# Down projections of a decoder layer: low and high input halves as one 512-column moving operand

## The reference, cut to what matters

```
def swiglu(h, w_gate, w_up, w_down):
    return (jax.nn.silu(h @ w_gate) * (h @ w_up)) @ w_down

x = x + 0.5 * swiglu(rms_norm(x, norm_ffn1), ffn1_gate, ffn1_up, ffn1_down)
...    # attention and RWKV mixing between the two
x = x + 0.5 * swiglu(rms_norm(x, norm_ffn2), ffn2_gate, ffn2_up, ffn2_down)
return rms_norm(x, norm_final)
```

## Time and profile before

| | |
|---|---|
| three runs | 624.00, 624.55, 629.41 us, median 624.55 |
| span of the profiled execution | 622.4 us |
| own time of the profiled execution | not in the record; the median stands 2.15 us above the span |
| PE busy | 98% of the span |
| two down projections | about 134 to 195 us and 554 to 615 us |

### The profile page before, as it was taken

The page is one execution under the profiler, slowest core; times in us unless marked ns, Lnnn a source line. Parts: engine busy times, 40 slices in busy tenths (PEclk is TensorE's granted clock), DMA queues, the critical chain, the costliest instruction groups (busy, mean ns, idle before and its releaser), DMA issues.

```text
span 622.4 us, 15455 instructions
## 1 busy us (share of the span) xinstructions
PE 612.2 (98%) x6716; PEld 597.0 (96%) x6716; DVE 421.0 (68%) x493; ACT 296.9 (48%) x345; POOL 89.4 (14%) x90
## 2 busy tenths in 40 slices
PE   9999999999999999999999999999999999999996
PEld 8899999999999999999988889999999999999996
DVE  5757787765556369968994336977767666665663
ACT  6734555444434274434665544644644444443332
POOL 0116900000114000020005524004000000000130
PEclk9999999999999999999999999999999999999999
DMA  8677656656555345585232222365566656556551
GB/s 287 217 229 236 201 183 186 191 169 200 177 189 200 98 136 190 190 187 159 91 120 87 71 86 77 103 201 183 179 196 202 202 185 187 186 170 208 181 166 67
DMA packets 100672, 105.40 MB, mean 169 GB/s; under 512 B 2244, under 2 KB 98732, under 8 KB 100628
## 3 DMA queue, kind: packets, MB, share of 16 engines
q1 hardware_dynamic: 99380, 101.47, 50.9%
q0 software_dynamic: 1088, 3.02, 2.2%
q10 hardware_dynamic: 160, 0.27, 0.1%
HBM read 103.50 MB, written 1.25 MB: 168 GB/s over the span
## 4 chain that ended last, share of the span: by engine, by line
PE 83%; DVE 8%; ACT 4%; DMA 3%; issue 1%; SPq 0%; ACTq 0%; DVEq 0%
PE two L1467 24%; PE two L1468 23%; PE two L1469 23%; PE two L1463 10%; DVE w_lo L905 4%; ACT w_hi L532 2%; DMA w_raw<-in_ffn_up 1%; DMA w_raw<-in_ffn_down 1%; DMA w_raw<-in_ffn_gate 1%; DMA x_tok<-in_x 1%; PE two L1741 1%; PE two L1742 1%; PE two L1743 1%; DVE gates L1110 0%; PE two L1886 0%
## 5 line engine op out<-in xcount | busy, mean ns | idle before, releaser
L532 ACT ACTIVATE w_hi<-w_raw 128x2048 fp32r<-128x2048 f32 (+1 forms) x86 | 162.5, 1890 | 244.4 <-PE two L1469 214.8
L905 DVE TENSOR_TENSOR w_lo<-w_raw,w_hi 128x2048 fp32r<-128x2048 f32 (+1 forms) x86 | 199.5, 2320 | 84.0 <-ACT w_hi L532 83.7
L1467 PE MATMUL two<-hlo_f,w_hi 128*128 128x256 f32 x640 | 177.8, 278 | 1.7 <-DVE w_lo L905 1.7
L1468 PE MATMUL two<-hhi_f,w_lo 128*128 128x256 f32 x640 | 177.4, 277 | 0.0
L1469 PE MATMUL two<-hhi_f,w_hi 128*128 128x256 f32 x640 | 177.4, 277 | 0.0
L1467 PEld LDWEIGHTS two<-hlo_f,w_hi 128*128 128x128 f32 x640 | 120.8, 189 | 2.7 <-DVE w_lo L905 2.2
L1468 PEld LDWEIGHTS two<-hhi_f,w_lo 128*128 128x128 f32 x640 | 120.9, 189 | 0.0
L1469 PEld LDWEIGHTS two<-hhi_f,w_hi 128*128 128x128 f32 x640 | 120.9, 189 | 0.0
L1467 PE MATMUL two<-hid_lo_t,w_hi 128*128 128x256 f32 x352 | 97.7, 278 | 0.7
L1468 PE MATMUL two<-hid_hi_t,w_lo 128*128 128x256 f32 x352 | 97.2, 276 | 0.0
L1469 PE MATMUL two<-hid_hi_t,w_hi 128*128 128x256 f32 x352 | 97.2, 276 | 0.0
(11 more groups left out here) (344 smaller groups left out, 981.9 us busy)
## 6 DMA issues: line engine op xcount, KB each, us to landing
w_raw<-in_ffn_up SPq DMA_DIRECT2D x21, 1024.0 KB, 5.4
w_raw<-in_ffn_gate SPq DMA_DIRECT2D x20, 1024.0 KB, 5.4
w_raw<-in_w_in SPq DMA_DIRECT2D x20, 1024.0 KB, 5.0
w_raw<-in_ffn_down SPq DMA_DIRECT2D x16, 896.0 KB, 4.6
w_raw<-in_ffn_down SPq DMA_DIRECT2D x8, 1024.0 KB, 5.0
w_raw<-in_w_out SPq DMA_DIRECT2D x4, 1024.0 KB, 5.0
w_raw<-in_proj_a SPq DMA_DIRECT2D x4, 512.0 KB, 3.7
w_raw<-in_proj_b SPq DMA_DIRECT2D x4, 512.0 KB, 4.3
```

The source lines that it names most:

```text
L532: nc.scalar.activation(whi[slot][:, 0:kts], raw[slot][:, 0:kts], ACT.Copy).then_inc(sg["hi_ready"], 1)
L905: nc.vector.tensor_tensor(wlo[slot][:, 0:kts], raw[slot][:, 0:kts], whi[slot][:, 0:kts].bitcast(F32), ALU.subtract).then_inc(sg["lo_ready" ...
L1467: mm(dst, whi[slot][:, k_, cols], xl, start=start, stop=False)
L1468: mm(dst, wlo[slot][:, k_, cols], xh, start=False, stop=False)
```

## The change

`hid_hi` and `hid_lo` become the two halves of one tile, `hid_x[P, FT, 2, T]`, with the low part first. For each 128-row tile the two products with the same high weights are one product with 512 moving columns, [low | high], into the whole bank. The product of the low weights with the high input goes to the bank's second half. The bank then holds two partial sums, so DVE adds each half of the bank to the residual by an instruction of its own, the second behind a semaphore that the first raises.

```
-            hid_hi = sb("hid_hi_t", [P, FT, T], F32R, scope=sc)
-            hid_lo = sb("hid_lo_t", [P, FT, T], F32R, scope=sc)
+            hid_x = sb("hid_x", [P, FT, 2, T], F32R, scope=sc)
+            hid_lo, hid_hi = hid_x[:, :, 0], hid_x[:, :, 1]
...
                             nc.vector.scalar_tensor_tensor(out=x[:, 2 * j + m], in0=bank[2 + m][:, 0:T], scalar=0.5,
                                                            in1=x[:, 2 * j + m], op0=ALU.mult, op1=ALU.add)\
+                                .then_inc(sg["x_half"], 1)
+                            dve.wait_ge(sg["x_half"], 2 * (j + f * (D // W)) + m + 1)
+                            nc.vector.scalar_tensor_tensor(out=x[:, 2 * j + m], in0=bank[2 + m][:, T:2 * T], scalar=0.5,
+                                                           in1=x[:, 2 * j + m], op0=ALU.mult, op1=ALU.add)\
                                 .then_inc((sg["x_ffn_even"], sg["x_ffn_odd"])[m], 1)
...
                             for c in range(KS[part_]):
-                                last = three(bank[2 + m][:, 0:T], s, c, slice(m * P, (m + 1) * P),
-                                             hid_hi[:, k0 + c], hid_lo[:, k0 + c],
-                                             k0 + c == 0, k0 + c == FT - 1)
+                                cols = slice(m * P, (m + 1) * P)
+                                part(bank[2 + m], whi[s][:, c, cols], hid_x[:, k0 + c].rearrange("p a t -> p (a t)"),
+                                     k0 + c == 0)
+                                last = part(bank[2 + m][:, T:2 * T], wlo[s][:, c, cols], hid_hi[:, k0 + c])
```

More of the change, by code:

```diff
@@ L124 @@
 first_hi first_lo first_norm sq_one sq_sum last_sq mean_sq rms_ready rstd_ready gained hhi_ready hlo_ready
-gate_taken up_taken silu_done hid_prod hid_hi hid_lo down_first x_ffn_even x_ffn_odd
+gate_taken up_taken silu_done hid_prod hid_hi hid_lo down_first x_half x_ffn_even x_ffn_odd
 bias_row bias_row_sb bias_out bias_in
```

## The result

The changed kernel takes 631.2 us in the median of 6 runs (627.8 to 635.92), the kernel before 624.27 us in the same comparison (6 runs, 621.42 to 629.41). The ratio is 1.009, with a 95% interval of 1.0046 to 1.0135: 3 to 8 us slower, where 2.6 us faster was forecast. The measured time lies outside the range.

What follows compares the result with a forecast made beforehand. PE's stream was taken as the bound. Products 3.77, first chunks -0.30, second-layer stalls -1.22, first-layer stalls +0.82 and end -0.46 summed to 2.61 us faster: 624.55 to 621.9 us, range 619.8 to 626.0.

Steps and rivals of the forecast that it cites:

- What bounds the kernel: Whole kernel: PE, busy 98% of the span at full clock, holds 83% of the chain; only shortening its stream gains.
- Products: Down projections: a tile goes from 340.0 to 329.3 ns (216 plus 113.3), 3.77 us faster over 352 tiles.
- the 216 ns passes: Eight plain-float32 passes of 256 columns, 216 ns each, 2.6 over streaming; taken as the price of a 512-column product.
- the cost goes by columns: Rival, down projections: the 6.7 ns belongs to each 256 columns, products gain nothing; 0.7 us slower, 625.2; chance 0.09.
- First chunks: First layer's third chunk, stall at 143.8: PE's gain in the two chunks before is lost waiting for late weights; -0.30 us.
- Additions and what stands behind them: DVE after groups 1 and 2: direct waits hidden; first layer's stalls vanish, +0.82 us; second layer's grow, -1.22 us.
- E + 2.36: Second layer: gain multiplication's predicted end, 2.36 us after E, PE's start of the next group's part 0.
- End: End of the kernel: the new addition stands whole in the final chain; -0.46 us.
- five stalls: Late chunk starts in the down projections, some 0.41 us each: one at 143.8, four after groups 1 and 2.
- I am wrong if the two steps of a tile sum to more than 332: Down projections: forecast refuted if a tile's steps sum above 332 or below 327 ns, or first layer's stalls stay.

Runs made afterwards that it cites:

- e3: The changed kernel with its products reordered: within a part and half, first all 512-column products, then all 256-column ones; ratio to the kernel before 1.0067.
- e5: The changed kernel without the 256-column products of the low weights, so its down projections have 512-column products alone; 613.03 us in one run.
- after_again: The changed kernel, unchanged, run again for a second trace; 631.63 us in one run.
- e4: The changed kernel with the first of the two additions per half left out; ratio to the kernel before 1.0097.
- e2: The kernel before with only the second addition per half added, of 0.0 times the bank; ratio 0.9996.
- e8: The kernel before with POOL's squaring after groups 1 and 2 waiting for DVE's low part of the next group's second chunk; median 622.93 us, ratio 0.9965.
- e7: The changed kernel with 44 warm-up products after the first down projection, putting later scan instructions where the kernel before has them; 639.14 us in one run.

## Why the prediction was wrong, point by point

**What bounds the kernel:** right. PE's stream sets the time, and all that was gained or lost went through it. Only "the full clock throughout" is not quite so: the granted clock was 0.5 from 29.0 to 32.5 us, which the page's tenths don't show. The down projections ran at 1.00.

**Products: wrong, and this is the step that failed.** I took 216 ns for the wide product because it "has the shape of the 216 ns passes", and 113.3 for the narrow one. The passes in the earlier trace rows are plain float32, which spends two cycles on a column, and have 2.6 ns over their streaming time. That surplus does not carry over to float32r at one cycle per column. There the surplus grows with the columns: 13 ns at 384, and 20 to 22 in the mean at 512 in three kernels with three different neighbourhoods (e3, e5 and the change). I had this as the rival "the cost goes by columns" and gave it 0.09. Even that rival was too mild, since it kept 340 ns per tile. The wide product never went below 225 ns, two at the lower price, and mostly took 235, two products at the higher price; and the narrow one beside it took 118. The tile is 353 instead of 329.3, and 352 tiles cost 352 x 13 = 4.6 us where a gain of 3.77 was booked. The records of 512 columns are 397 ns long, not 380.

The surplus of 6.7 ns which I read as a loss between two equally long activities is the lower of two prices of 256 columns. The first trace happens to show the lower one in nearly all long stretches, so the step looked like a constant. In all twelve traces a stream of 256-column products changes between the two prices only at a break: a late start, another shape, or, in after_again at 50.4 us, a single step of 124 ns. The unbroken stream behind it keeps its price, and the mixed stream of the change is at the higher one but for single wide products right behind a break.

The Trainium skill ("TensorE: Matmul & The Clock Gate", section Back-to-back issue gap) has N / 2.4 + 2.5 for an isolated product, 215.8 ns for 512 columns. The float32 passes of the earlier trace rows, with the same 213.3 ns of streaming, come near it at 216. No float32r product here does; the least that any kernel showed for 512 columns is 225.

**First chunks:** the term (-0.30) assumed a gain to lose. In the first trace the late weights were hidden instead, and that stall went too. In the second the stall was there (0.38 us at 145.16), so the term is 0 to +0.4 by the execution.

**Additions and what stands behind them:** the direct waits are hidden, as worked out. For the first layer the mechanism was right, too: the low part takes its turn before POOL's addition, and the stalls go (+0.82 booked, two stalls of 0.41 gone; by e4 the longer part alone would have hidden half of that). For the second layer it was right in kind and wrong in order. I had the low part ready at E + 2.36, 0.07 us after POOL's addition (-1.22). In truth DVE started it 0.07 us before the record of the gain multiplication ends, at 590.01 where POOL's addition has 590.02, and had the turn: +0.82 in place of -1.22. e2 shows it without the wide products, and e8 shows the mechanism from the other side. The rule behind it is in the Trainium skill ("SBUF — State Buffer", section SBUF: two separate sides): an exclusive lock for the whole instruction, which goes to the one that starts first. The traces agree: the low part, with two inputs in SBUF, and POOL's addition stand one behind the other, and the loser's time grows by what is left of the winner's, to within 0.2 us (1.30 to 3.15 behind 2.01 in e2).

**End:** +0.46, as booked.

**What no step had:** the pauses of PE in the scan. The change takes 88 products and their loads out of the body of a loop ahead of it, which moves all later instructions of PE's program. In these two pairs of traces that costs 2.4 us, a little under half of the measured loss. e7 shows that the place in the program causes it, and that it isn't tied to wide products as such. The prediction had this term at nothing and gave no reason.

Together: +4.6 for the products, -2.0 for five stalls (-1.6 where the first stays), +0.46 at the end, +2.4 in the scan is 5.5 us, where the ratio gives 5.6 with an interval from 2.9 to 8.4. That the two agree to a tenth is luck: a gate and up stage that draws the higher price moves a run by 4 us. The forecast's own condition, "I am wrong if the two steps of a tile sum to more than 332", was met.

## What to carry to other kernels

Joining two products that share their weights saves a load, and a load that is already hidden is worth nothing: look at what the step has over its pure streaming time, and whether that surplus was measured in the same data type. A surplus of 6% in a long regular stream may be one of two levels and not a constant; look for the other one in the trace (the kernel before has 118 ns from start to start at 201 to 211 us, in the products with lora_whi and lora_wlo) before booking it as something that a change removes. And a change that takes instructions out of one engine's program moves everything behind it: compare the traces where the diff does nothing, too.

## What the runs showed of the hardware that I had not expected

- 256 float32r columns with 128x128 weights take 113.3 or about 117.7 ns from start to start, at the full granted clock (1.00). Stretches of over 900 products ran at the higher price in one execution and at the lower in another. In the gate and up stage of the second layer that is 120.8 against 125.1 us. The price is drawn at a break of the stream and then kept; what decides the draw is open.
- These draws go a long way to explain the scatter between the traces. From its first product to the down projection, the first gate and up stage took 122.6 to 123.2 us in six traces, 126.1 to 127.0 in five, and 125.0 in the one with the low clock. e2 (span 619.2) and e8 (625.7) differ by 6.5 us, of which 4.4 lie in this stage and 1.9 in the first down projection, mostly at the lower price in e2 and at the higher in e8.
- At a granted clock of 0.5 the surplus is gone: 256 columns took 213 ns (before, from 29.0 us) and 512 took 427 (e5, from 184.0 us).
- At the full clock 512 columns took 225 to 226, 231 or 235 to 236 ns, 384 columns mostly 170 to 177: steps of some 5 ns.
- PE pauses inside streams that wait for no semaphore (start to start 0.4 to 1.4 us), at places fixed by the program, some 1.4 us behind the landing of a 16 KB packet on the instruction queue. 176 more instructions of PE ahead moved four such pauses away.
- In the second layer, whether DVE or POOL goes first was decided by differences of 0.18 us or less between their issues (the earlier trace rows against e2), and the second one then waited for the whole instruction.
